# Pairwise sums ahead of the statistics matmuls, and the last two FFN down projections joined

## The reference, cut to what matters

```
h   = modulate(rmsnorm(x, norm1_g), sh1, sc1)
p   = h @ w_in                                   # 1024 -> 4608
u   = dwconv31(glu(p[conf])) + b ; u = silu(layernorm(u)) ; y_a = u @ conf_w_out
v   = g_b * dwconv3(g_c * v)     ; y_b = v @ sc_w_out
x   = x + gt1 * ((ga * y_a + gb * y_b) @ w_o)
h2  = modulate(rmsnorm(x, norm2_g), sh2, sc2)
x   = x + gt2 * ((silu(h2 @ w_g) * (h2 @ w_u)) @ w_down)     # 1024 -> 2816 -> 1024
out = rmsnorm(x, final_g)
```

## Time and profile before

| | us |
|---|---|
| median of 3 runs (lowest, highest) | 935.91 (935.80, 936.46) |
| the profiled execution | 935.88 |
| its slowest core's span (others 932.0 to 933.5) | 934.3 |
| TensorE busy, share of the span | 887.2, 95% |
| VectorE busy | 464.2, 50% |
| ScalarE busy | 316.8, 34% |
| GpSimd busy | 50.6, 5% |

### The profile page before, as it was taken

The page is one execution under the profiler, slowest core; times in us unless marked ns, Lnnn a source line. Parts: engine busy times, 40 slices in busy tenths (PEclk is TensorE's granted clock), DMA queues, the critical chain, the costliest instruction groups (busy, mean ns, idle before and its releaser), DMA issues.

```text
span 934.3 us, 13266 instructions; the slowest of 8 cores (932.0 to 934.3 us)
## 1 busy us (share of the span) xinstructions
PE 887.2 (95%) x4476; PEld 402.9 (43%) x4476; DVE 464.2 (50%) x693; ACT 316.8 (34%) x487; POOL 50.6 (5%) x73
## 2 busy tenths in 40 slices
PE   3598999999999999999999999999999999999994
PEld 0143444444444444444444444444444444444453
DVE  3855646667666565746541221562115521235587
ACT  3565766555422222237731111001110011100364
POOL 0012200000000000000010000000000000000022
PEclk9699999999999999999999999999999999999997
DMA  8976489331667626292016112240122211110045
GB/s 267 287 184 174 103 137 173 84 79 34 170 140 271 175 91 158 57 231 74 0 31 106 34 34 46 46 80 14 21 46 45 46 35 35 34 34 1 1 166 196
DMA packets 29156, 91.94 MB, mean 98 GB/s; under 512 B 3233, under 2 KB 13729, under 8 KB 24866
## 3 DMA queue, kind: packets, MB, share of 16 engines
q1 hardware_dynamic: 23474, 59.13, 20.6%
q0 software_dynamic: 5184, 31.57, 19.6%
q10 hardware_dynamic: 432, 0.39, 0.1%
HBM read 105.73 MB, written 8.39 MB: 122 GB/s over the span
## 4 chain that ended last, share of the span: by engine, by line
PE 88%; DMA 5%; SPq 2%; DVE 2%; issue 1%; ACT 1%; POOL 0%; DVEq 0%; POOLq 0%; ACTq 0%
PE ps L350 68%; PE ps L956 15%; DMA arena<-wada 3%; PE ps L646 3%; SPq L419 2%; DMA arena<-w 1%; PE ps L511 1%; DVE arena L336 1%; DMA arena<-xc 1%; ACT arena L329 1%; POOL arena L460 0%; PE ps L443 0%; SPq L365 0%; DVE arena L332 0%; DVEq L139 0%
## 5 line engine op out<-in xcount | busy, mean ns | idle before, releaser
L350 PE MATMUL ps<-arena 128*128 128x512 bf16 (+1 forms) x3044 | 667.1, 380 | 8.1 <-DMA arena<-cb 2.7
L350 PEld LDWEIGHTS ps<-arena 128*128 128x128 bf16 (+1 forms) x3044 | 297.9, 98 | 369.3 <-issue 13.2
L332 DVE TENSOR_TENSOR arena<-ps,arena 128x512 bf16<-128x512 f32 (+1 forms) x156 | 107.7, 691 | 308.3 <-PE ps L350 226.0
L336 DVE SCALAR_TENSOR_TENSOR arena<-ps,arena 128x512 f32<-128x512 f32 (+2 forms) x216 | 156.5, 729 | 93.1 <-PE ps L956 42.7
L329 ACT ACTIVATE arena<-arena 128x512 bf16<-128x512 f32 (+4 forms) x226 | 139.5, 650 | 160.1 <-DVE arena L336 92.5
L329 ACT ACTIVATE arena<-ps 128x512 f32<-128x512 f32 x110 | 65.2, 594 | 303.2 <-PE ps L350 303.0
L956 PE MATMUL ps<-arena 128*128 128x512 bf16 (+1 forms) x752 | 159.4, 368 | 0.0
L329 ACT ACTIVATE arena<-ps,arena 128x512 f32<-128x512 f32 (+1 forms) x125 | 81.8, 687 | 127.2 <-PE ps L350 115.9
L956 PEld LDWEIGHTS ps<-arena 128*128 128x128 bf16 x752 | 74.2, 99 | 79.6
L332 DVE TENSOR_TENSOR arena<-arena 128x512 f32<-128x512 f32 (+3 forms) x138 | 91.3, 685 | 32.1 <-ACT arena L329 17.9
L336 DVE SCALAR_TENSOR_TENSOR arena<-arena 128x512 f32<-128x512 f32 (+2 forms) x66 | 50.6, 774 | 22.3 <-ACT arena L329 18.4
(11 more groups left out here) (19 smaller groups left out, 49.1 us busy)
## 6 DMA issues: line engine op xcount, KB each, us to landing
arena<-wada SPq DMA_DIRECT2D x48, 512.0 KB, 7.9
arena<-w POOLq DMA_DIRECT2D x21, 1024.0 KB, 10.6
arena<-arena SPq DMA_DIRECT2D x64, 130.0 KB, 2.7
arena<-xc SPq DMA_DIRECT2D x8, 1024.0 KB, 9.8
arena<-xc SPq DMA_DIRECT2D x4, 2048.0 KB, 16.9
arena<-wd POOLq DMA_DIRECT2D x8, 768.0 KB, 8.0
outT<-arena SPq DMA_DIRECT2D x24, 256.0 KB, 2.5
arena<-w POOLq DMA_DIRECT2D x6, 512.0 KB, 9.3
```

Of the source, the lines that this page charges most:

```text
L332: sch.op(eng, lambda e: e.tensor_tensor(out=out, in0=in0, in1=in1, op=op), reads=reads, writes=writes)
L336: sch.op("dve", lambda e: e.scalar_tensor_tensor(out=out, in0=in0, scalar=scalar, in1=in1, op0=op0, op1=op1), reads=reads, writes=writes)
L350: fns.append(lambda e, lt=lt, rh=rh, i=i: e.matmul(bank[b], lhsT=lt, rhs=rh, start=(i == 0), stop=(i == n - 1)))
```

## The change

Three things are different.

1. In `conv_a` the casts are gone. When an odd channel tile is done, VectorE adds the f32 pair (j - 1, j) into `cbf[j]` as bf16 and the pair of squares in place into `csq[j]`. `st_a` has two ones-matmuls over each, four in all.
2. In `norm_pipe`, mode 2, squares are added in pairs by VectorE (`add_pairs`, called in the unit after the second square, behind that unit's residual update), and `red` runs over the four sums. It runs one unit after the sum was issued (lag 1). In the final mode nothing is paired.
3. `down_stage(2)` and `down_stage(3)` become `down_last`: each unit has twelve matmuls into one bank, over both groups, and one residual update. It has the pieces of the old last stage, so group 2 is now halved in the last position tile too. The lag is 2 (3 for halves). The four slots hold the halves of both groups at once. The final norm has temporaries of its own (`NT_F`, in the place of the unused part of `hbuf`) and a ring of 8 output tiles; GpSimd takes k = 1 and 5 of the last piece only.

```diff
-        NOT = 16
+        NOT = 8
+        NT_F = norm_temps(94208, (O_H + 16384 - M, O_H + 24576 - M), "f")
...
-                if k in ((1, 4, 6) if last else (2, 6)):
+                if last and k in (1, 5):
                     TT(ot, xk, rstd, ALU.mult, [B_x, B_rstd], [B_ot[o]], eng="pool")
...
+            pair = mode != "final"
+            NS = KD // 2 if pair else KD
+            left = [NS] * len(pieces)
...
+            def add_pairs():
+                while adds:
+                    m, pi = adds.pop(0)
+                    s, n = (pi % 2) * 8 + m, pieces[pi][2]
+                    TT(t.sq[s][:, 0:n], t.sq[s - 1][:, 0:n], t.sq[s][:, 0:n], ALU.add, [t.B_sq[s - 1], t.B_sq[s]], [t.B_sq[s]])
+                    reds.append((m, pi))
+
             for (m, pi) in order:
                 unit(m, pieces[pi])
-                if len(reds) >= (lag if pieces[pi][2] == TU else lag + 1):
+                if len(reds) >= (1 if pair else lag if pieces[pi][2] == TU else lag + 1):
                     red(*reds.pop(0))
+                add_pairs()
                 sq(m, pi)
-                reds.append((m, pi))
+                if pair:
+                    if m % 2 == 1:
+                        adds.append((m, pi))
+                else:
+                    reds.append((m, pi))
                 pop(pops)
...
-                    if state["u"] == 1:
+                    add_pairs()
+                    if state["u"] == 2:
                         while reds:
                             red(*reds.pop(0))
...
-                    sch.op("dve", lambda e, j=j: e.tensor_copy(out=cbf[:, j * TU:(j + 1) * TU], in_=c32[:, j * TU:(j + 1) * TU]),
-                           reads=[B_c32[j]], writes=[B_cbf[j]])
+                    if j % 2 == 1:
+                        TT(cbf[:, j * TU:(j + 1) * TU], c32[:, (j - 1) * TU:j * TU], c32[:, j * TU:(j + 1) * TU], ALU.add,
+                           [B_c32[j - 1], B_c32[j]], [B_cbf[j]])
+                        TT(csq[:, j * TU:(j + 1) * TU], csq[:, (j - 1) * TU:j * TU], csq[:, j * TU:(j + 1) * TU], ALU.add,
+                           [B_csq[j - 1], B_csq[j]], [B_csq[j]])
...
-                        MM(bb, [(ones_c, src[:, j * TU:(j + 1) * TU]) for j in range(4)], list(B_src) + [B_cst])
+                        MM(bb, [(ones_c, src[:, j * TU:(j + 1) * TU]) for j in (1, 3)], [B_src[1], B_src[3], B_cst])
...
+            def down_last():
+                s = [wd_slot(g, half) for half in range(2) for g in (2, 3)]
+                parts = [(2, [s[0], s[2]]), (3, [s[1], s[3]])]
+                pieces = [(r, 0, TU) for r in range(NR - 1)] + [(NR - 1, 0, 256), (NR - 1, 256, 256)]
+                norm_pipe(pieces, [(m, pi) for pi in range(len(pieces)) for m in range(KD)],
+                          lambda m, p: down_unit(parts, m, p), "final", lag=2)
...
             gu_stage(3)
-            down_stage(2, False)
-            down_stage(3, True)
+            down_last()
```

More of the change, by code:

```diff
@@ L468, in norm_apply @@
         def norm_apply(p, pi, k, mode, last=False):
-            t = NT_N
+            t = NT_F if mode == "final" else NT_N
             r, c0, n = p
@@ L497, in norm_pipe @@
         def norm_pipe(pieces, order, unit, mode, filler=None, pops=1, lag=2):
-            t = NT_N
-            left = [KD] * len(pieces)
-            reds, tasks = [], []
+            t = NT_F if mode == "final" else NT_N
+            pair = mode != "final"
+            NS = KD // 2 if pair else KD
+            left = [NS] * len(pieces)
+            reds, adds, tasks = [], [], []
             def sq(m, pi):
@@ L508, in red @@
                 n, b, s = pieces[pi][2], 6 + pi % 2, (pi % 2) * 8 + m
-                first, last = left[pi] == KD, left[pi] == 1
+                first, last = left[pi] == NS, left[pi] == 1
                 left[pi] -= 1
@@ L937, in gu_stage @@
                         gu_unit(g, j, r)
-            def down_stage(g, last):
-                j0, j1 = FGROUPS[g]
-                nk = j1 - j0
-                slots = []
-                for half in range(2):
-                    slot = ffn_slots[fs["i"] % 4]
-                    fs["i"] += 1
-                    load_slot(slot, wd_d[g * 2 + half], ncols=3072)
-                    slots.append(slot)
-                def unit(m, p):
-                    r, c0, n = p
-                    slot = slots[m // 4]
-                    b = next_bank()
-                    out = bank[b][:, 0:n]
-                    prs = [(slot_ap[slot][:, kk * 512 + (m % 4) * 128: kk * 512 + (m % 4 + 1) * 128],
-                            abuf[g % 2][:, kk * S + r * TU + c0: kk * S + r * TU + c0 + n]) for kk in range(nk)]
-                    sch.pe_group([lambda e, lt=lt, rh=rh, kk=kk: e.matmul(out, lhsT=lt, rhs=rh, start=(kk == 0), stop=(kk == nk - 1))
-                                  for kk, (lt, rh) in enumerate(prs)],
-                                 reads=[B_ab[g % 2][kk][r] for kk in range(nk)] + [slot_buf[slot]], writes=[B_bank[b]])
-                    xk, B_x = xpiece(m, p)
-                    STT(xk, out, mod[:, 40 + m:41 + m], xk, ALU.mult, ALU.add, [B_bank[b], B_mod, B_x], [B_x])
-                if not last:
-                    for m in range(KD):
-                        for r in range(NR):
-                            unit(m, (r, 0, TU))
-                else:
-                    pieces = [(r, 0, TU) for r in range(NR - 1)] + [(NR - 1, 0, 256), (NR - 1, 256, 256)]
-                    norm_pipe(pieces, [(m, pi) for pi in range(len(pieces)) for m in range(KD)], unit, "final", lag=3)
@@ new lines, in wd_slot, with down_unit @@
+            def wd_slot(g, half):
+                slot = ffn_slots[fs["i"] % 4]
+                fs["i"] += 1
+                load_slot(slot, wd_d[g * 2 + half], ncols=3072)
+                return slot
+            def down_unit(parts, m, p):
+                r, c0, n = p
+                b = next_bank()
+                out = bank[b][:, 0:n]
+                prs, rd = [], []
+                for (g, slots) in parts:
+                    j0, j1 = FGROUPS[g]
+                    slot = slots[m // 4]
+                    rd += [B_ab[g % 2][kk][r] for kk in range(j1 - j0)] + [slot_buf[slot]]
+                    prs += [(slot_ap[slot][:, kk * 512 + (m % 4) * 128: kk * 512 + (m % 4 + 1) * 128],
+                             abuf[g % 2][:, kk * S + r * TU + c0: kk * S + r * TU + c0 + n]) for kk in range(j1 - j0)]
+                nk = len(prs)
+                sch.pe_group([lambda e, lt=lt, rh=rh, kk=kk: e.matmul(out, lhsT=lt, rhs=rh, start=(kk == 0), stop=(kk == nk - 1))
+                              for kk, (lt, rh) in enumerate(prs)], reads=rd, writes=[B_bank[b]])
+                xk, B_x = xpiece(m, p)
+                STT(xk, out, mod[:, 40 + m:41 + m], xk, ALU.mult, ALU.add, [B_bank[b], B_mod, B_x], [B_x])
@@ new lines, in down_stage @@
+            def down_stage(g):
+                parts = [(g, [wd_slot(g, 0), wd_slot(g, 1)])]
+                for m in range(KD):
+                    for r in range(NR):
+                        down_unit(parts, m, (r, 0, TU))
+            def down_last():
[4 more added lines that the diff above has]
+                          lambda m, p: down_unit(parts, m, p), "final", lag=2)
```

6 lines of the change are left out of this document (3 added, 3 removed).

## The result

| us | before | after |
|---|---|---|
| median of the runs shown | 936.01 | 926.79 (5 runs; the two lowest 924.29 and 924.60) |
| ratio to before, with its 95% interval | | 0.9882 [0.9867, 0.9897], so 925.0 us |
| the profiled execution | 935.88 | 926.79 |
| its slowest core's span (others) | 934.3 (932.0 to 933.5) | 925.1 (921.2 to 922.3) |

In two of the five runs after (1057 and 1071 us) four cores ran 117 to 148 us longer than the others at a lower granted clock; they pull the median up, and the ratio leaves them out. The change makes the kernel 1.2% faster, 11.0 us, against the 11.3 us forecast.

What follows compares the result with a forecast made beforehand. TensorE was taken to bound the kernel, VectorE the stretch at its end. Gains of 3.0 (convolution), 1.95 (second norm), 4.4 (joined groups) and 2.0 (end) sum to 11.3 us: 935.9 to 924.6 us, range 921.8 to 929.0.

Steps and rivals of the forecast that it cites:

- What bounds the kernel: Whole kernel: TensorE carries the chain, so each 512-column matmul removed returns 0.216 us; VectorE binds the stretch at the end.
- Convolution: Convolution statistics: 16 fewer ones-matmuls save 3.45 us, less 0.4 waiting in the first tile; gain 3.0 us, bounds 2.2 to 3.45.
- Norm 2: Second norm: 16 fewer ones-matmuls save 3.45 us, less one 1.5 us wait behind the table load; gain 1.95 us.
- the sum of two bf16 tiles: VectorE's pair sum of squares: taken as 0.55 us for 512 elements, with 0.42 as lower and 0.69 as upper bound.
- The joined units: Last two FFN groups: twelve-matmul half units take 1.42 us against VectorE's 1.06, so waits and slow clock go; gain 4.4 us.
- the slow clock: Last half units: TensorE's granted clock of 0.90 should return to 1.00 to the end of the units once they are joined.
- The end: After the last unit: first scaling 1.9 us sooner, scalings 0.1 us shorter; gain 2.0 us, bounds 1.0 to 2.5.
- The range's low end: Whole kernel: 921.8 us, if there is no wait in the norm and the end comes out best.
- A: Final norm: waits stay because VectorE's order, not its load, makes them; 4.4 and 1.9 us lost, 930.9 us; chance 0.08.
- B: Second norm: the new 1.5 us wait lowers the clock, costing 1.7 us, 926.3 us; chance 0.11.
- C: Second norm: every pair sum makes TensorE wait, 12 pairs by 0.7, 8 us, 932.6 us; chance 0.05.
- D: Fifth joined unit: the fourth weight slot's load may land late, TensorE waiting up to 24 us, 948 us; chance 0.04.

Runs made afterwards that it cites:

- e9: The changed kernel, with squares also added in pairs in the three full pieces of the final norm: 922.49 us, ratio 0.9845 to the kernel before.
- e1: The kernel before, with the convolution's pair sums alone: 935.65 us, ratio 1.0004; gain by distance 2.1 us.
- e2: The kernel before, with the pair sums of the second norm alone: 934.39 us, ratio 0.9986; gain by distance 1.8 us.
- e6: The kernel before, with only the final norm's edits (lag 2, 8 output tiles, GpSimd in k = 1 and 5 of the last piece): 934.53 us, ratio 0.9988.
- e5: The changed kernel, with the final norm as before (lag 3, 16 output tiles, old GpSimd share): 924.89 us, ratio 0.9881 to the kernel before.
- e8: The changed kernel, with the last weight load issued twice into the same slot so it lands later: 932.75 us, ratio 0.9962 to the kernel before.
- e4: The changed kernel, with the second norm's ones-matmuls one pair sum later (lag 2 for 1): 922.05 us, ratio 0.9853 to the kernel before.
- e12: The changed kernel with lag 2 in norm 2, pair sums in the final norm's full pieces, and no GpSimd in the final norm: 919.43 us, ratio 0.9821.

## Why the prediction came out right, point by point

**What bounds the kernel.** Right. A matmul that was taken away returned its 0.216 us where nothing else was late (twelve of them in e9: 2.6), and nothing where something was (the convolution's last tile).

**Convolution, forecast 3.0 us, measured 2.1.** The step that failed is "Does anything wait for these sums? In the first tile yes", with three tiles taken as free. The sums themselves came out as said: the first tile waits 1.23 - 0.96 = 0.27 longer (0.4 forecast; both groups wait together instead of the second after the first). But I looked only for who waits for the *sums*. The gate units wait for a chain on VectorE and ScalarE that is as long in both kernels, and TensorE waited for it before by 0.05 us, so the last tile had nothing to give. From 3.45 go 0.27 and the last tile's 0.86: 2.3, against 2.1 by distance (e1).

**Norm 2, forecast 1.95, measured 1.8** (e2). The mechanism was right in each link: table load, rstd, multiplication, residual update, sum. The wait costs 1.43 us from start to start (1.27 listed), against 1.5. One term of it was too large, the sum of two bf16 tiles, for which I took 0.55 from the 4096-element row. The group of after in which every such sum stands:

```profile
L333 DVE TENSOR_TENSOR arena<-arena 128x512 bf16<-128x512 bf16 x24 | 10.0, 416 | 0.0
```

0.42 us, as the lower bound. The estimate near 0.4 by the rule of the Trainium skill (VectorE: DVE Perf Modes, The perf-mode tier table) would have been the better value, and the trace agrees with it. The gain closes: 3.45 less 1.43 for the wait and 0.36 for the gap behind the norm, plus 0.15 for two short stops of before that are gone, is 1.8.

**The joined units, forecast 4.4, measured 4.6 on the slowest core and 4.0 on most.** From the first matmul of the last stage to the end of its last unit it was 94.04 us before and 89.45 after, on the slowest cores. That core is not typical: by matmul starts the stretch is 94.2 us on cores 5 and 7 of before and 93.6 on the other six, where more backlog is left behind the last unit, and 89.6 on all after. Units stand as forecast; the chain of after on core 6, first in the full and then in the half pieces:

```profile
834.53 2.59 PE ps L976 x12
837.34 2.59 PE ps L976 x12
...
907.75 1.31 PE ps L976 x12
909.17 1.31 PE ps L976 x12
```

2.81 and 1.42 us apart, without a wait. Before, half units were shorter than what VectorE does for each; now they are longer (1.42 against 1.06). e6 shows the other half of this: without the joining the rhythm stays at 1.05. One part of the mechanism is not borne out: the slow clock went, as said, but it had cost the stage nothing, since VectorE set its end.

**The end, forecast 2.0, measured 2.6 on the slowest cores and 3.5 by medians.** To the first scaling 4.79 became 2.99 on the slowest cores, and 1.9 was forecast: right but for 0.1. By medians 5.5 became 3.0, since most cores had more backlog. The scalings took 3.40, as forecast. Not forecast was what is gained behind the last scaling: 0.6 us on the slowest cores, 0.9 by medians. e5 and e6 show that it comes with the edits of the final norm; which of them, the ring or the order of the last stores, was not separated.

**The sum is partly luck.** By distance it is 2.1 for the convolution, 1.8 for norm 2, 4.0 and 3.5 for the last stage, 11.4 to 11.6 us, and 11.0 by the ratio. The convolution's 0.9 too much and the last stage's 1.1 too little cancel, which is why 11.3 was met. The range's low end, 921.8, is also 0.4 below what its terms give (11.3 + 1.5 + 0.45 + 0.5).

**The rivals.** A: fell; with longer units the waits are gone (e5 has the old lag of 3 and none, e6 the new lag and keeps them). Its mechanism is there all the same: the scaling that waits for the norm does stop VectorE (1.58 us before), and a longer unit covers it. The cover before was also larger than I wrote: the lag for halves was 4, so 3.1 us and not 2.3. B: fell; the clock stayed at 1.00 behind 1.27 us of idle TensorE, while behind 5.9 us it was 0.50 (e8). Its price, taken from the earlier trace rows, was one core's: four cores kept 1.00 behind the same waits. C: fell; one wait, not twelve, and VectorE was busy 44 of 65 us. D: did not happen, but by 1.5 to 3.0 us only, and e8 shows the price when it does.

## What to carry to other kernels

A matmul that is taken from a full TensorE is worth its length only up to the next place where TensorE meets a chain on the other engines. Follow such chains from the edited place to the next join, and compare their length with TensorE's work beside them: here the join was 29 us away. A sum that is put between a square and its ones-matmul, in a queue that can block, needs a lag of two sums; with one TensorE waited (e4: 1.8 us). And where a follower needs longer per unit than the unit takes, merging two accumulations into one unit removes the waits and half of the follower's work at once.

## What the runs showed of the hardware

- A single wait of 1.27 us did not lower the granted clock. In e8 waits of 4.7 to 6.8 us did on all eight cores, and 0.50 stayed for some microseconds of full work behind it, at a cost of 2.1 us on core 4. At the end of the kernel before, waits of 1.6 to 1.7 and 0.73 us close together lowered it on some cores of one execution and not on others; 0.48 and 0.65 in e6 did on none.
- The slow TensorE clock at the end of the kernel before cost nothing, as VectorE set the pace there: the stage took 97.5 us to the last ones-matmul on all eight cores, with it and without.
- A scaling of 256 columns takes VectorE 0.41 us alone. With GpSimd multiplying beside it, six took 3.40 us (e12 against after). A scaling of 512 columns took 1.85 us beside GpSimd and 0.75 alone (before against e6).
- The last weight load, 768 KB, landed 7.1 to 8.6 us behind its issue over the cores of after.
- Cores of one execution reach the same instruction up to 4.5 us apart after the first loads. A difference below that can be read from distances inside a core, and not from the slowest span.
